# Third block's recurrence, head norms and attention: marks of the dense lane counted from its led steps

## What is computed

```python
h = rmsnorm_3(x, norm_mix_g[l]);  z = h @ w_in[l]
(fq, fk, fv, ff, hq, hf, hi, hg, ca, cb, gl) = jnp.split(z, IN_SPLITS, axis=-1)
qa = rmsnorm_3(split_heads(fq, FOX_HEADS), fox_q_norm_g[l])      # norms of the heads
logf_a = jax.nn.log_sigmoid(ff + fox_forget_b[l])                # forget gate, summed along the sequence
ya = fox_attention(qa, ka, va, logf_a)                           # attention, six heads of 64
yb = hgrn2_chunkwise(hq, kb_in, hi, logf_b)                      # recurrence, four heads, in chunks of 64
yb = rmsnorm_3(yb, hgrn_out_norm_g[l]) * jax.nn.silu(hg)
yc = jax.nn.silu(layernorm_3(causal_dwconv(ca * jax.nn.sigmoid(cb), ...)))
gates = jax.nn.sigmoid(gl + gate_b[l])                           # three gates of 1024 columns
merged = gates[0] * (ya @ wb[0]) + gates[1] * (yb @ wb[1]) + gates[2] * (yc @ wb[2])
```

## Time and profile before

| | |
|---|---|
| median of 3 runs | 2956.51 us (2954.5 to 2956.64) |
| profiled execution | 2952.26 us, its span 2950.5 us |
| busy: TensorE, weight loads | 2834.2 us (96%), 2316.5 us (79%) |
| busy: VectorE, GpSimd, ScalarE | 1390.4 us (47%), 1221.6 us (41%), 1136.9 us (39%) |
| DMA | 274.71 MB, mean 93 GB/s |
| recurrence phase after its led steps | 2224.9 to 2336.8 us |
| norms phase after its led steps | 2347.8 to 2408.7 us |
| attention phase after its led steps | 2419.8 to 2484.9 us |

### The profile page before, as it was taken

The page is one execution under the profiler, slowest core; times in us unless marked ns, Lnnn a source line. Parts: engine busy times, 40 slices in busy tenths (PEclk is TensorE's granted clock), DMA queues, the critical chain, the costliest instruction groups (busy, mean ns, idle before and its releaser), DMA issues. The chain is left out here.

```text
span 2950.5 us, 39994 instructions
## 1 busy us (share of the span) xinstructions
PE 2834.2 (96%) x16029; PEld 2316.5 (79%) x16029; DVE 1390.4 (47%) x2505; ACT 1136.9 (39%) x2060; POOL 1221.6 (41%) x586
## 2 busy tenths in 40 slices
PE   6999999999999989999999999999998899999998
PEld 4865568888988877777889989988797667888887
DVE  6336650341043362774544555532587553565620
ACT  4357762222244333443554422222343455522221
POOL 5432224454444432222223545554445423555553
PEclk9999999999999998999999999999999999999999
DMA  7410003223322211112324322233222223422332
GB/s 268 145 56 16 15 30 100 99 94 100 112 96 93 95 60 59 44 44 99 122 68 134 131 89 93 93 100 107 82 95 84 77 75 130 138 93 93 101 103 90
DMA packets 84088, 274.71 MB, mean 93 GB/s; under 512 B 9727, under 2 KB 9983, under 8 KB 83776
## 3 DMA queue, kind: packets, MB, share of 16 engines
q1 hardware_dynamic: 82568, 271.32, 27.7%
q10 hardware_dynamic: 1336, 0.83, 0.1%
HBM read 257.36 MB, written 17.90 MB: 93 GB/s over the span
## 5 line engine op out<-in xcount | busy, mean ns | idle before, releaser
L135 POOL TENSOR_TENSOR weights_lo<-weights_raw,weights_hi 128x1024 fp32r<-128x1024 f32 x413 | 1002.7, 2430 | 1345.0 <-ACT weights_hi L127 1344.6
L127 ACT ACTIVATE weights_hi<-weights_raw 128x1024 fp32r<-128x1024 f32 x413 | 435.3, 1058 | 1041.4 <-PE acc L548 440.5
L546 PE MATMUL acc<-h_hi,weights_hi 128*128 128x512 f32 (+1 forms) x1096 | 436.7, 398 | 21.9 <-POOL h_lo L1441 6.7
L548 PE MATMUL acc<-h_hi,weights_lo 128*128 128x512 f32 (+1 forms) x1096 | 424.1, 387 | 0.0
L547 PE MATMUL acc<-h_lo,weights_hi 128*128 128x512 f32 (+1 forms) x1096 | 423.9, 387 | 0.0
L546 PEld LDWEIGHTS acc<-h_hi,weights_hi 128*128 128x128 f32 x1096 | 208.6, 190 | 77.7 <-issue 32.0
L548 PEld LDWEIGHTS acc<-h_hi,weights_lo 128*128 128x128 f32 x1096 | 208.2, 190 | 41.8
L547 PEld LDWEIGHTS acc<-h_lo,weights_hi 128*128 128x128 f32 x1096 | 208.6, 190 | 36.4 <-issue 0.2
L546 PE MATMUL acc<-h,weights_hi 128*128 128x258 f32 (+2 forms) x592 | 186.0, 314 | 6.7 <-ACT gate_tiles L2652 3.4
L547 PE MATMUL acc<-h,weights_hi 128*128 128x258 f32 (+2 forms) x592 | 173.0, 292 | 0.0
L548 PE MATMUL acc<-h,weights_lo 128*128 128x258 f32 (+2 forms) x592 | 172.7, 292 | 0.0
(11 more groups left out here) (474 smaller groups left out, 6348.8 us busy)
## 6 DMA issues: line engine op xcount, KB each, us to landing
weights_raw<-in_stream SPq DMA_DIRECT2D x413, 512.0 KB, 3.3
weight_ring<-in_w_ada SPq DMA_DIRECT2D x24, 512.5 KB, 8.3
gates<-gate_tiles SPq DMA_DIRECT2D x24, 258.0 KB, 4.1
gate<-gates SPq DMA_DIRECT2D x8, 774.0 KB, 5.4
held<-gates SPq DMA_DIRECT2D x8, 768.0 KB, 5.8
gates<-gate_tiles SPq DMA_DIRECT2D x23, 256.0 KB, 4.0
bias_copies<-bias_rows SPq DMA_DIRECT2D x1, 3068.0 KB
table<-bias_copies SPq DMA_DIRECT2D x1, 2560.0 KB, 9.9
```

The source lines that it names most:

```text
L127: act.activation(self.hi[:, at % CUT, :], self.raw[:, at % RAW, :], ACT.Copy).then_inc(self.hi_done, 1)
L135: pool.tensor_tensor(self.lo[:, at % CUT, :], self.raw[:, at % RAW, :], self.hi[:, at % CUT, :].bitcast(F32), ALU.subtract).then_inc(self. ...
L546: pe.matmul(out, left[0], right[0], start=start, stop=False)
L548: return pe.matmul(out, left[1], right[0], start=False, stop=stop)
```

## The change

In three phases of the third block the begin of the dense lane's span changes from 0 to `ahead(dense, 2 * KT)`, which is -16/81, -16/49 and -16/41: the marks of the 16 led steps lie before 0, and the marks of the rest spread over 0 to 1. Nothing else is touched: the instructions, buffers and semaphores are the same, and only the places of the dense steps among the companions' slots differ, on all five queues.

```diff
-                run.lanes(paced((dense.weights, 0, 1), (heads.weights, 0, 1), ([1], 1, 1)), [dense, heads, StoredGates(store)], 2 * KT)
+                run.lanes(paced((dense.weights, ahead(dense, 2 * KT), 1), (heads.weights, 0, 1), ([1], 1, 1)), [dense, heads, StoredGates(store)], 2 * KT)
...
-            run.lanes(paced((dense.weights, 0, 1), (forget.weights, 0, 0.8), (fox_norm.weights, 0, 0.9), (head_norm.weights, 0, 0.75),
+            run.lanes(paced((dense.weights, ahead(dense, 2 * KT), 1), (forget.weights, 0, 0.8), (fox_norm.weights, 0, 0.9), (head_norm.weights, 0, 0.75),
                                 (conv_norm.weights, 0, 1), (gated.weights, 0.8, 1), ([1], 1, 1)),
...
-            order = paced((dense.weights, 0, 1), (attention.weights, 0, 1), ([1] * (packed + CONV_TILES), 0.2, 0.8), ([1], 1, 1))
+            order = paced((dense.weights, ahead(dense, 2 * KT), 1), (attention.weights, 0, 1), ([1] * (packed + CONV_TILES), 0.2, 0.8), ([1], 1, 1))
```

## The result

The changed kernel takes 2960.89 us (median of 20 runs, 2953.88 to 2963.68), the kernel before 2954.82 us (median of 20 runs, 2950.42 to 2959.66): a ratio of 1.0017, with a 95% interval of 1.0011 to 1.0022. So it is slower by 5 us by the ratio and by 6 by the medians, where a faster kernel was forecast, at 2949.2 us, and the time lies just above the range of 2940 to 2960. The 20 times of the changed kernel fall into two clusters, 4 from 2953.9 to 2955.7 us at a mean granted clock of 0.983 to 0.984, and 16 from 2959.0 to 2963.7 us at 0.980 to 0.981.

What follows compares the result with a forecast made beforehand. TensorE, busy 96%, was taken as the bound, waiting on VectorE and ScalarE at the phases' heads. Recurrence -3.8, norms -1.5 and attention -2.0 gave -7.3 us from the median 2956.51: 2949.2 us, range 2940 to 2960.

Steps and rivals of the forecast that it cites:

- The frame: After the three phases TensorE is full, so each microsecond they give or take arrives at the end one to one.
- the seams: Transitions between phases cost nothing; ahead of the attention, 8.8 us of cover stand against a tail later by less than 2.
- (a): Recurrence: the first query product starts later, behind three more dense steps and a rounding on ScalarE; plus 2.3 us.
- (b): Recurrence: VectorE's waits for TensorE and ScalarE shrink from 11.1 to 5.7 us, minus 5.4; bounds nothing or all 11.1.
- the bound of +1.6: Upper bound of the recurrence's sum of minus 3.8 us; the lower bound was -9.5.
- 92.1 us of work, which stays: Recurrence: VectorE's 103.2 us window less its waits leaves 92.1 us of work, taken as unchanged by the new order.
- rival 2: Slower, as VectorE and GpSimd take turns in the recurrence's first head, which grows by 5.2 us; 2961.3 us, chance 0.11.
- (c): Recurrence's end: 4 dense steps instead of 5 between the last level's product and the last slot; minus 0.7 us.
- The signs that I named: Signs of error: later heads still 27 to 28 us with VectorE busy throughout, or a long squares wait with 1.2 GHz behind.
- Norms, -1.5: Norms: dense steps moved to the head shorten TensorE's waits for ScalarE's squares; minus 1.5 us, bounds +2 and -5.6.
- my 4.1: Norms: TensorE's remaining waits for squares, 1.0 + 0.6 + 2.5 = 4.1 us, instead of 5.6.
- Attention, -2.0: Attention: dense steps cover four row-minima waits, minus 2.4, with some +0.4 at the end; minus 2.0 us, bounds 0 and -2.8.

Runs made afterwards that it cites:

- the execution of 124.7 us: Profiled execution with the changed dense-step order in the recurrence only, norms and attention as in the kernel before; the kernel measured 2962.46 us, ratio 1.0017.
- short rests: GpSimd's recurrence rests cut to 128 of 1024 columns: 2946.18 us (0.9968) in the order of before, 2943.20 us (0.9959) in the changed order.
- the tail was covered: Only the norms changed against the kernel before, plus three dense steps moved in TensorE's order ahead of the Fox norm's last spread product: 2954.86 us, 0.9998.
- the norms alone: The change applied only in the norms, recurrence and attention as in the kernel before: 2958.82 us, ratio 1.0009.

## Why the prediction was wrong, step by step

**The frame held.** Behind the phases nothing was given back (465.6 us in both), and the seams cost nothing.

**Recurrence, (a) the later start: right.** The chain on ScalarE came as I had laid it out: rounding, table load, 1.16 us to the first decay. The first query product stands 15.5 us behind the first led step (2228.40 against 2212.88) where it stood 12.9: +2.6, forecast +2.3.

```profile
2224.14 1.06 ACT L127 ACTIVATE weights_hi<-weights_raw 128x1024 fp32r<-128x1024 f32 x1 [3.90 <-PE acc L548]
2225.22 1.28 ACT L3289 ACT_TABLE_LOAD   x1
2226.51 0.63 ACT L3289 ACTIVATE q_in<-sums 128x512 f32<-128x512 f32 x1
...
2228.40 1.82 DVE L3365 TENSOR_TENSOR q_part<-held,decay 128x512 f32<-128x512 f32 x1 [0.62 <-ACT decay L3299]
```

**(b) VectorE's waits from 11.1 to 5.7: right at full clock only, the second step that failed.** In the execution of 124.7 us they are 6.0 (3.1, 0.6 and 2.3). In the changed kernel's profile they are 11.1. The 7 us lie between two executions of one order that agree up to the first drop of the clock, so this part is shown to be the clock's. The sum put the low clock at nothing, and the bound of +1.6 had no low clock in it, though the earlier trace rows showed the price of one in the same phase.

**"92.1 us of work, which stays": this is the step that failed.** VectorE's instructions are the same, but their time includes being blocked by GpSimd, and that depends on what meets what. It grew by 6.3 to 6.7 us. (Of the 92.1 us in the profile before, VectorE was busy 90.0; the rest are small gaps. And that profile is the shorter of two kinds: four others of the same order show 93.1, so against them the growth is 3.3 to 3.7.) By group, before and then after:

```profile
L3357 DVE TENSOR_TENSOR apart<-sums 128x256 f32<-128x256 f32 x22 | 17.9, 814 | 0.0
L3356 DVE TENSOR_TENSOR apart<-sums 128x256 f32<-128x256 f32 x22 | 13.7, 624 | 0.3
...
L3377 DVE TENSOR_TENSOR kd<-kd,hf 128x512 f32<-128x512 f32 x4 | 3.8, 951 | 0.0
```

```profile
L3356 DVE TENSOR_TENSOR apart<-sums 128x256 f32<-128x256 f32 x22 | 17.9, 812 | 0.3
...
L3357 DVE TENSOR_TENSOR apart<-sums 128x256 f32<-128x256 f32 x22 | 12.4, 565 | 0.0
L3377 DVE TENSOR_TENSOR kd<-kd,hf 128x512 f32<-128x512 f32 x4 | 8.1, 2037 | 0.0
...
L3337 DVE TENSOR_TENSOR kd<-sums 128x512 f32<-128x512 f32 x3 | 4.1, 1369 | 0.1
```

The last group took 2.1 us before. The two lines of `apart` lose 1.3 us between them, the products of L3377 and L3337 gain 6.3. The `kd` product of a head took 0.95 us on average; in the new order it meets a rest in the first and in the last head (2.84 and 2.86 us), and TensorE's two longest waits, 3.48 and 2.82 us, stand right behind these meetings. Against rival 2 I had argued that what the first head gains in blocking the others lose, since the rests are as many. The trace agrees with the rule of the Trainium skill that I cited there ("SBUF — State Buffer", Who interferes with whom), 2.84 us beside a rest of 2.80, but not with my inference from it that the sum would stay: a GpSimd instruction costs VectorE only what VectorE has ready beside it, and at times that is nothing (the two lengths of the old order, below, show such a case).

Rival 2 and the objection to it looked at the rests alone. Count each VectorE instruction against the shortest of its kind, and put the excess down to the GpSimd instruction that overlaps it most: beside the rests it goes from 11.1 to 13.6 us, beside GpSimd's own work for the recurrence, the `k_part` products (L3322), from 13.3 to 17.0. In the profiles of 125.7 us it is 13.1 and 14.6, and with short rests 1.1 and 12.9 before, 1.4 and 17.8 after. So the larger part of the new blocking lies beside `k_part`. It begins with the first query product, shown above at 2228.40 with 1.82 us, which now starts together with

```profile
2228.37 2.97 POOL L3322 TENSOR_TENSOR k_part<-hf,decay 128x512 f32<-128x512 f32 x2 [0.71 <-ACT decay L3299]
```

and took 0.69 us before, behind it. By balance, in the execution of 124.7 us, which lost 1.7 us of clock: start +2.0, VectorE's work +6.7, its other time -6.1, end -0.8, together +1.8 us (124.7 against 122.9). The short rests show the other side: with the long rests gone, the same marks gave 3.0 us.

**(c) one step less at the end, -0.7: right**, 6.8 us from the last take to the next phase became 6.1.

**Rival 2** had the sign, the +2.3, and the first head near 28 us (28.9). Its mechanism was half of it: VectorE and GpSimd do take turns, at other instructions and in all heads, and the larger part in most executions, 7.0 us, is the clock behind TensorE's waits. The signs that I named spoke accordingly: later heads of 27.1 to 30.1 us, a granted clock of 0.50 at 2240.

**Norms, -1.5: wrong in the phase, right in its head.** The waits for squares came to 1.8 us, better than my 4.1. The Fox norm's fifth square was done within 0.5 us of where I had put it (counted from the phase's first led step), but TensorE reached it 1.6 us later than I had reckoned and waited 1.4 us instead of 2.5, and the waits of 1.0 and 0.6 before it came to 0.36. The half clock that I priced at 1.8 us cost nearly nothing: the same order takes 71.9 us with it and 71.7 without. The tail, which stood in the bound (+2) and not in the sum, took 2.6. Net +1.1 in the changed kernel, -1.0 once the tail was covered.

**Attention, -2.0: the sign right, the size half.** Some -1.0 on average. Where the clock stays, the phase takes 76.1 us instead of 76.2, though TensorE's waits fell from 2.4 to 1.4 us, so counting them at their length was the error.

**The advice to interleave** (the Trainium skill, "Perfetto Trace Analysis", Optimization Strategy) says that performance may be improved by interleaving stretches with different limits. Here, spreading the dense steps over the recurrence cost 5 us while VectorE and GpSimd held each other up more; with short rests it gave 3.0.

**What stays open.** Why the clock falls behind a wait in one execution and not in another of the same order was not found; no profile shows a cause ahead of the drop. How much of the recurrence's 5 us is the start and how much the order is bounded only loosely. And no run takes the blocking beside `k_part` away, so its share of the 5 us is read from traces, not from an experiment.

**The two lengths of the old order** show how the clock and the blocking act on each other. Its recurrence took 122.9 us with a clock loss of 3.4, and 125.7 with 1.7. The executions agree up to a wait of 2.72 us. First the kernel before, then the norms alone (its recurrence is the old one):

```profile
2232.74 2.05 PE L3227 MATMUL pair_acc<-q_part,k_part 128*128 128x128 f32 x8 [2.72 <-DVE q_part L3365]
...
2236.24 0.42 DVE L3357 TENSOR_TENSOR apart<-sums 128x256 f32<-128x256 f32 x1
```

```profile
2231.23 1.13 PE L3227 MATMUL pair_acc<-q_part,k_part 128*128 128x128 f32 x8 [2.72 <-DVE q_part L3365]
...
2235.51 2.58 DVE L3357 TENSOR_TENSOR apart<-sums 128x256 f32<-128x256 f32 x1
```

Where the clock fell, GpSimd's next rest began 5.9 us after this product instead of 4.0, and VectorE's subtraction was through before it. Where the clock stayed, the same subtraction met the rest, and TensorE then waited 2.46 us for the next query product. So more low clock went with a phase that was 2.8 us shorter, and the kernel's profile on which the prediction rests happened to be one of the short ones.

## What to carry to other kernels

When an edit only moves work between in-order queues, the durations read from the trace are not all constants: list which instructions of VectorE lie beside a GpSimd instruction in the new order, and put the blocked time into the sum with its own bound. Look at all of GpSimd's instructions, not only at the longest. Steps that fill TensorE's waits at the head of a phase are taken from its tail, so look for the longest VectorE instruction there before moving them. And where TensorE waits in several places, compare phase lengths over several executions, because the clock may add several microseconds in some and nothing in others.

## What the runs showed of the hardware

- One order of instructions ran the recurrence in 124.7 or 131.7 us. Around a wait of 3.48 us the granted clock stayed at 1.00 in one execution and fell to 0.50 in the two others; in the former it fell behind a later wait of 2.07 us. In the old order it fell around a wait of 2.72 us in two executions and stayed in four.
- What a low clock cost depended on the place: a clock loss of 1.7 us went with 1.2 us more in the attention and 0.2 in the norms with the old marks, and 1.7 us more of it in the old recurrence with 2.8 us less.
- VectorE's busy time in the recurrence, with the same 135 instructions, was 90.0 or 93.1 us in executions of the old order and 96.3 to 96.7 in the new one; the excess lay beside GpSimd's instructions.
- With a GpSimd subtraction of 1024 columns split into two of 512, VectorE got in between them (held up by at most 1.1 us instead of 2.2), was held up more often (12 times instead of 7), and lost as much in total (12.1 us against 11.1 and 13.1).
